# Key convolution of a delta head moved into the tail of the head before it, query gate and value taps moved ahead of the inversion

## The chip, the cores and the metric

The kernel runs on one core of one Trainium2 chip. The metric is the device time of one execution in microseconds (us). In what follows TensorE is the matmul engine (PE in the rows, PEld its weight loads), VectorE is DVE, ScalarE is ACT, and SP is the queue that issues the weight transfers.

## The reference

One step of a two-layer hybrid model in float32, for 1024 prompt tokens and 8 sample tokens (1032 columns here). Layer 0 mixes with four gated-delta heads and four retention heads, layer 1 with four mLSTM heads; each layer ends with a squared-ReLU MLP. The change touches the delta heads alone:

```python
proj = xn @ w_in
conv_out = silu(causal_conv(qkv_a, conv_buf, w_conv))      # 4 taps per channel
q, k, v = split(conv_out); q = l2norm(q) * DK**-0.5; k = l2norm(k)
beta = sigmoid(b_raw); log_alpha = -exp(a_log) * softplus(a_raw + dt_bias)
# per chunk of tokens, g = cumsum(log_alpha):
a_mat = I + (k*beta @ k.T) * decay_strict;  u, w = solve(a_mat, [v*beta, k*beta*exp(g)])
qk = (q @ k.T) * decay_causal
# over the chunks, with the state S:
v_new = u - w @ S;  o = (q*exp(g)) @ S + qk @ v_new;  S = S*exp(g_last) + k_dec.T @ v_new
o = rmsnorm(o, gdn_gain) * silu(g_a)
```

## The kernel before

**Work and its order.** Everything is laid out with channels on the 128 partitions and tokens along the free dimension. A projection tile is one 128-channel output, 8 blocks of 128 input channels deep, in three thirds of 344 tokens. The weights and inputs are split in a high and a low part, so one step (one block of one third) is three matmuls, and a tile is 24 steps. Each third fills one of three banks of `PJ`, and VectorE drains it (`project_steps`, L851); a third may start only when the third three before it is drained. After a tile's last third VectorE splits the weights of a later tile (L804, the cast, and L807, the low part).

**Heads and weaving.** Layer 0 has eight units: delta heads are units 0 to 3, retention heads 4 to 7. While unit u is computed, TensorE also runs the four tiles v of u, then gate, k and q of u+1: 96 steps. They fill the places at which the head's generator yields. `DELTA_FILL` says how many steps run at each named place, and the same names and numbers let VectorE's `weave` work out after which place a third is due (one per 8 steps). Each engine has one instruction queue in program order. Engines tell each other by counting semaphores: `to_act`, `to_dve`, `to_pe` and `act_to_pe`, each waited for by the next number (`n.awaited`). A plain `n.awaited(to_dve)` only counts one signal past.

**Banks.** Five more PSUM banks carry everything else. TensorE's `claim(b, reader)` waits until the bank's last reader has emptied it; `publish` hands it over; the reader's `take` and `done` answer.

**The front of a delta head, before.** TensorE puts row sums of the gates into banks 1, 2, 4, 3 and 0 and yields `start`, `keys conv`, `keys gate` (7, 10 and 8 steps). It then waits for ScalarE's squares of k, sums them over the partitions into banks 1, 2 and 4 (L409), puts masked row sums into banks 3 and 0 (L428 and L432), and yields `keys norm` (11 steps). Then it waits for the normalised k, forms k·k per chunk (L422) and transposes k (L419). VectorE meanwhile does k's three older taps (`conv(1)`: L966 three times, L970), the output gate (L962), `silu(1)` (L981), q's taps, the k scaling (L1004), and LT from k·k (L1008). ScalarE does the newest tap of k and q (L1654), the gate's tanh (L1664), the decays (L1660) from banks 1 and 2, k's tanh (L1668), small exps from bank 4 (L1671, L1672), k's squares (L1674), a table load (L1675), the exps of banks 3 and 0 (L1678), and the reciprocal root of the sums (L1586, L1589).

**The inversion.** Seven levels; at each, TensorE makes two halves of level products, two of block products and two of transposes, with VectorE masking or copying after each (L1082, L1101, L1111). VectorE puts into it `silu(0)` after level 1's masks, v's three taps around levels 1 and 2, and q's scaling and products at levels 3 and 4. No projection steps are placed inside.

**The tail.** After the scan over the chunks TensorE yields `rows`, `output` and `outer` (7, 10 and 11 steps) around a sample outer product. VectorE adds it to the sample state (L1196); then it normalises and gates the head's output (L1210, L1211). ScalarE stores both states (L1618). The next head begins on ScalarE with a wait that VectorE releases, then one for both stores to have landed, then the load of the next state (L1650) and the newest tap of k.

## Time and profile before

| | |
|---|---|
| median of 3 runs | 2789.54 us (2787.52 to 2790.8) |
| profiled execution, its own time | 2787.88 us |
| its span, first to last instruction | 2785.9 us |
| TensorE busy | 2719.1 us, 98% of the span |
| VectorE busy | 1550.8 us, 56% |
| ScalarE busy | 433.0 us, 16% |
| mean granted TensorE clock | 0.992 of full |

The delta heads lie between 59 and 491 us of the span, about 108 us each. Head 0 starts at 59.2 us, and the outer products that close heads 0, 1, 2 and 3 start at 166.0, 274.9, 383.0 and 491.2 us. TensorE is counted busy while any matmul is in flight.

### The profile page before, as it was taken

The page shows a single profiled execution, that of the slowest core. Times are in us where ns is not written, and L with a number is a line of the kernel's source. Part 1 is how long each engine was busy: PE and PEld are TensorE (multiplying, and loading weights), DVE is VectorE, ACT ScalarE, POOL GpSimd, SP SyncE. Part 2 cuts the span into 40 slices and gives each one's busy share as a digit, 9 for nine tenths or more (in the row PEclk, how much of TensorE's full clock was granted, in tenths as well). Part 3 has the DMA queues.
Part 4 walks back from the last instruction along what each step waited for, and adds up shares of the span by engine and source line. Part 5 has one row for each costly group of instructions (what it writes and reads, how often), then busy time and mean ns, then how long its engine had stood idle before and what let it go on. Part 6 is the DMA issues. An engine that isn't in the chain of part 4 may idle for free. (4 is left out here: it accounts for less than half of the span.)

```text
span 2785.9 us, 41603 instructions
## 1 busy us (share of the span) xinstructions
PE 2719.1 (98%) x17354; PEld 2644.0 (95%) x17354; DVE 1550.8 (56%) x2850; ACT 433.0 (16%) x894; POOL 0.2 (0%) x4
## 2 busy tenths in 40 slices
PE   8999999999899999999999999999999999999998
PEld 8888888899899999999999999999899999999998
DVE  8665765556676355364466535445675264462563
ACT  5451442222230000000001121223220000000001
POOL 0000000000000000000000000000000000000000
PEclk9999999999999999999999999999999999999999
DMA  3010011111211111111112112102311111111111
GB/s 139 16 40 17 31 47 39 52 60 60 100 41 47 53 46 46 46 46 49 48 49 92 61 38 71 68 27 77 116 40 52 46 46 46 46 46 53 46 61 61
DMA packets 44986, 150.94 MB, mean 54 GB/s; under 512 B 6024, under 2 KB 11016, under 8 KB 43792
## 3 DMA queue, kind: packets, MB, share of 16 engines
q1 hardware_dynamic: 33984, 115.42, 12.4%
q10 hardware_dynamic: 10832, 32.99, 3.2%
q8 instruction: 138, 2.26, 0.3%
q14 instruction: 32, 0.26, 0.0%
HBM read 130.32 MB, written 18.08 MB: 53 GB/s over the span
## 5 line engine op out<-in xcount | busy, mean ns | idle before, releaser
L351 PE MATMUL proj<-x_hi,w_hi 128*128 128x344 f32 x4572 | 1489.8, 326 | 18.2 <-DVEq L859 8.4
L351 PE MATMUL proj<-x_hi,w_lo 128*128 128x344 f32 x4572 | 1464.3, 320 | 0.0
L351 PE MATMUL proj<-x_lo,w_hi 128*128 128x344 f32 x4572 | 1463.7, 320 | 0.0
L351 PEld LDWEIGHTS proj<-x_hi,w_hi 128*128 128x128 f32 x4572 | 863.8, 189 | 33.6 <-issue 25.6
L351 PEld LDWEIGHTS proj<-x_lo,w_hi 128*128 128x128 f32 x4572 | 863.4, 189 | 1.7
L351 PEld LDWEIGHTS proj<-x_hi,w_lo 128*128 128x128 f32 x4572 | 863.3, 189 | 0.0
L1381 DVE TENSOR_TENSOR h<-h,proj 128x344 f32<-128x344 f32 x144 | 73.8, 512 | 372.3 <-PE proj L351 372.3
L807 DVE TENSOR_TENSOR w_lo<-w_raw,w_hi 128x1024 fp32r<-128x1024 f32 x195 | 239.0, 1226 | 7.9 <-DVE state L1147 0.7
L1366 DVE TENSOR_TENSOR mlp_t<-proj,rbc 128x344 f32<-128x344 f32 x192 | 99.0, 515 | 237.8 <-PE proj L351 224.1
L422 PE MATMUL bank<-s,s 128*128 128x128 f32 x1096 | 141.4, 279 | 14.8 <-DVE s L1040 4.5
L422 PEld LDWEIGHTS bank<-s,s 128*128 128x128 f32 x1096 | 129.3, 192 | 25.5 <-DVEq L785 8.9
L851 DVE TENSOR_TENSOR s<-proj,rbc 128x344 f32<-128x344 f32 x156 | 78.8, 513 | 118.2 <-PE proj L351 115.2
L804 DVE CAST w_hi<-w_raw 128x1024 fp32r<-128x1024 f32 x195 | 134.0, 687 | 4.3 <-DVE state L1147 1.2
L1596 ACT ACTIVATE ssq<-h 128x344 f32<-128x344 f32 x9 | 4.3, 481 | 635.6 <-DVE h L894 635.6
L1371 DVE TENSOR_TENSOR x_lo<-mlp_u,x_hi 128x344 fp32r<-128x344 f32 x192 | 99.4, 517 | 6.6
L1368 DVE SCALAR_TENSOR_TENSOR mlp_u<-mlp_t 128x344 f32<-128x344 f32 x192 | 99.3, 517 | 6.6
L1874 ACT ACTIVATE ssq<-h 128x344 f32<-128x344 f32 x3 | 1.4, 481 | 630.7 <-DVE h L1352 630.7
L1370 DVE CAST x_hi<-mlp_u 128x344 fp32r<-128x344 f32 x192 | 65.3, 340 | 6.5
L419 PE MATMUL bank<-consts,s 128*128 128x128 f32 x416 | 57.3, 277 | 6.2 <-DVEq L785 5.7
L419 PEld LDWEIGHTS bank<-consts,s 128*128 128x128 f32 x416 | 46.0, 141 | 13.7 <-DVEq L785 11.5
L1721 ACT ACTIVATE s<-bank 128x128 f32<-128x128 f32 x64 | 17.8, 278 | 258.5 <-PE bank L422 258.5
L966 DVE SCALAR_TENSOR_TENSOR s<-s,vec,s 128x1021 f32<-128x1021 f32 (+2 forms) x36 | 45.3, 1258 | 3.4 <-ACT s L1654 2.3
(323 smaller groups left out, 2021.8 us busy)
## 6 DMA issues: line engine op xcount, KB each, us to landing
w_raw<-w_all SPq DMA_DIRECT2D x204, 512.0 KB, 3.5
h<-x SPq DMA_DIRECT2D x8, 516.0 KB, 9.3
h<-x ACTq DMA_DIRECT2D x8, 516.0 KB, 6.9
h_spill<-h ACTq DMA_DIRECT2D x8, 516.0 KB, 2.6
h<-h_spill ACTq DMA_DIRECT2D x8, 516.0 KB, 5.6
y<-h SPq DMA_DIRECT2D x24, 172.0 KB, 1.9
sample_C<-state_c ACTq DMA_DIRECT2D x4, 1024.0 KB, 6.9
s_state_c<-sample_C ACTq DMA_DIRECT2D x4, 1024.0 KB
```

What stands on the lines that cost most here:

```text
L351: last = nc.tensor.matmul(PJ[:, tt, 0:TT], w[slot][:, k, :], x[:, k, tt * TT:(tt + 1) * TT], start=(at == 0 and j == 0), stop=(at == len(o ...
L419: per_chunk(b, reader, half, lambda o, c: nc.tensor.transpose(o, chunk(src, c), ident))
L422: return nc.tensor.matmul(o, l, r, start=start, stop=stop)
L804: nc.vector.tensor_copy(hi[:], src).then_inc(w_hi_done, 1)
L807: tt_(lo[:], src, hi[:].bitcast(F32), ALU.subtract).then_inc(w_split, 1)
L851: return tt_(third(dst, tt), ps, third(rbc, tt), ALU.mult)
L966: return stt(dst[:, sh:SEQ], src[:, 0:SEQ - sh], vcol(w + i), dst[:, sh:SEQ], ALU.mult, ALU.add)
L1366: drain(t, tt, lambda ps, tt: tt_(T_third[:], ps, third(rbc, tt), ALU.mult), g)
L1368: step(stt(U_third[:], T_third[:], 0.0, T_third[:], ALU.max, ALU.mult))
L1370: step(nc.vector.tensor_copy(hi, U_third[:]))
L1371: tt_(lo, U_third[:], hi.bitcast(F32), ALU.subtract).then_inc(x_ready, 1)
L1381: drain(t0 + 8 + c, tt, lambda ps, tt: tt_(hh, hh, ps, ALU.add), g)
```

## The change

Between the heads, the newest tap and the three older taps of the next head's k are done in the tail of the head ahead (head 0 still does its own at its front). The output's normalising and gating move from behind the sample outer product to in front of it, and for that VectorE waits there for the reciprocal root. Inside a head, ScalarE takes k's squares before the decays and small exps instead of after them, and q's tanh comes in front of the table load, the exps of banks 3 and 0 and the reciprocal root of k. `silu(0)`, v's newest tap, v's three older taps and q's squares go in front of the inversion; q's norm sums move from level 2 to level 1, its scaling and decayed product from level 3 to 2, and the q·k product from level 4 to 3. The fill becomes 14 steps at `start`, 10 at `keys conv`, 4 at `keys gate` and 8 at `keys norm`; TensorE's wait for k's squares now stands behind `start`, its k·k behind `keys gate`, and `keys norm` comes after the transposes of k. The diff:

```diff
@@ -68,7 +68,7 @@
-DELTA_FILL = {"start": 7, "keys conv": 10, "keys gate": 8, "keys norm": 11, "keys": 0, "invert": 1,
+DELTA_FILL = {"start": 14, "keys conv": 10, "keys gate": 4, "keys norm": 8, "keys": 0, "invert": 1,
               "level 0": 0, "level 1": 0, "block": 0, "turn": 0, "scan": 1, "state": 2, "residual": 1, "values": 1,
@@ -457,15 +457,14 @@
                     yield "start"
-                    yield "keys conv"
-                    yield "keys gate"
                     pe.wait_ge(*n.awaited(act_to_pe))
...
                         publish(hide_later(b), b)
-                    yield "keys norm"
+                    yield "keys conv"
+                    yield "keys gate"
                 else:
@@ -477,6 +476,7 @@
                         turned((4, 3)[half], "act", k, half)
+                    yield "keys norm"
                     yield "keys"
@@ -488,10 +488,10 @@
                             per_chunk(half, "dve", half, lambda o, c: mm(o, chunk(LT, c), chunk(Dm, c)))
-                        if lv == 2:
+                        if lv == 1:
                             pe.wait_ge(*n.awaited(act_to_pe))
                             over_partitions(ones, s[10], "act", (2, 4, 3))
-                        if lv == 4:
+                        if lv == 3:
                             pe.wait_ge(*n.awaited(to_pe))
@@ -961,20 +961,20 @@
-                def tap(x, i, src, dst):
+                def tap(x, i, src, dst, h=h):
                     w, sh = V_CONV + 4 * (x * HEADS + h), 3 - i
...
-                def earlier_rows(x, dst):
+                def earlier_rows(x, dst, h=h):
                     at = V_HIST + 3 * (x * HEADS + h) * NB
...
-                def conv(x):
+                def conv(x, h=h):
                     src, dst = s[x], s[4 + x]
...
                     for i in range(3):
-                        step(tap(x, i, src, dst))
-                    earlier_rows(x, dst).then_inc(*n.made(to_act))
+                        step(tap(x, i, src, dst, h))
+                    earlier_rows(x, dst, h).then_inc(*n.made(to_act))
@@ -990,23 +990,32 @@
                     q, k, vs, OT = s[4], s[5], s[6][:, SEQ:TOK], s[6]
-                    conv(1)
+                    if h == 0:
+                        conv(1)
+                    n.awaited(to_dve)
+                    gate()
+                    silu(1).then_inc(*n.made(to_act))
                     yield "start"
-                    gate()
-                    n.awaited(to_dve)
-                    silu(1).then_inc(*n.made(to_act))
-                    yield "keys conv"
                     for i in range(3):
...
                     earlier_rows(0, q).then_inc(*n.made(to_act))
+                    yield "keys conv"
+                    all_drained(T_AB + 4 * unit + 3)
+                    tell(to_act)
+                    silu(0).then_inc(*n.made(to_act))
                     yield "keys gate"
...
                     tt_(k[:], k[:], s[12][:], ALU.mult).then_inc(*n.made(to_pe))
+                    v.wait_ge(*n.awaited(to_dve))
+                    for i in range(3):
+                        step(tap(2, i, s[2], s[6]))
+                    step(earlier_rows(2, s[6]))
                     yield "keys norm"
...
                         tell(to_pe)
+                    tell(to_act)
                     yield "keys"
@@ -1074,7 +1083,6 @@
                     n.settle()
-                    all_drained(T_AB + 4 * unit + 3)
                     for lv in range(1, LEVELS):
@@ -1083,14 +1091,10 @@
                             yield "block"
-                        if lv == 1:
-                            silu(0).then_inc(*n.made(to_act))
                         if lv == 2:
-                            step(tap(2, 1, s[2], s[6]))
-                        if lv == 3:
                             v.wait_ge(*n.awaited(to_dve))
                             step(stt(q[:], q[:], QSCALE, s[10][:], ALU.mult, ALU.mult))
-                        if lv == 4:
+                        if lv == 3:
                             for half in range(2):
@@ -1114,13 +1118,7 @@
                                 yield f"level {half}"
-                        if lv == 1:
-                            v.wait_ge(*n.awaited(to_dve))
-                            step(tap(2, 0, s[2], s[6]))
                         if lv == 2:
-                            step(tap(2, 2, s[2], s[6]))
-                            earlier_rows(2, s[6]).then_inc(*n.made(to_act))
-                        if lv == 3:
                             tt_(s[10][:], q[:], s[7][:], ALU.mult).then_inc(*n.made(to_pe))
@@ -1188,6 +1186,14 @@
                     step(ts_(s[9][:, 0:NB * P], s[9][:, 0:NB * P], consts[:, K_RG + h:K_RG + h + 1], None, ALU.mult))
+                gain = vcol(V_GDN if delta else V_RET)
+                if delta:
+                    if h < HEADS - 1:
+                        all_drained(T_AB + 4 * unit + 5)
+                        tell(to_act)
+                    v.wait_ge(*n.awaited(to_dve))
+                    step(tt_(OT[:], OT[:], s[12][:], ALU.mult))
+                    step(stt(MIX[:, unit, :], OT[:], gain, MIX[:, unit, :], ALU.mult, ALU.mult))
                 yield "outer"
@@ -1195,8 +1201,12 @@
-                gain = vcol(V_GDN if delta else V_RET)
+                if delta:
+                    if h < HEADS - 1:
+                        all_drained(T_AB + 4 * unit + 6)
+                        tell(to_act)
+                        conv(1, h + 1)
+                    return
                 if unit == 2 * HEADS - 1:
@@ -1477,8 +1487,9 @@
             for u in range(2 * HEADS):
-                all_drained(T_AB + 4 * u + 3 - LATE[0])
-                tell(to_act)
+                if u == 0 or u >= HEADS:
+                    all_drained(T_AB + 4 * u + 3 - LATE[0])
+                    tell(to_act)
                 if u < 2 * HEADS - 1:
@@ -1648,7 +1659,7 @@
                 a.dma_start(s[9][:, 0:NB * P], io["state_a" if delta else "state_b"][h]).then_inc(state_in, 16)
-                def newest_tap(x):
+                def newest_tap(x, h=h):
                     act(convo[:, x * HEADS + h, 0:3 + NB], s[x][:, SEQ - 3:TOK], ACT.Copy)
@@ -1660,23 +1671,30 @@
-                    newest_tap(1).then_inc(*n.made(to_dve))
+                    if h == 0:
+                        newest_tap(1).then_inc(*n.made(to_dve))
+                    newest_tap(0).then_inc(*n.made(to_dve))
                     act(s[16][:], s[3][:], ACT.Tanh, scale=0.5).then_inc(*n.made(to_dve))
-                    newest_tap(0).then_inc(*n.made(to_dve))
-                    decays(s[17], 1, 0)
                     a.wait_ge(*n.awaited(to_act))
                     act(s[12][:], s[5][:], ACT.Tanh).then_inc(*n.made(to_dve))
+                    a.wait_ge(*n.awaited(to_act))
+                    act(s[12][:], s[5][:], ACT.Square).then_inc(*n.made(act_to_pe))
+                    decays(s[17], 1, 0)
                     decays(s[17], 2, 1)
...
                     a.wait_ge(*n.awaited(to_act))
-                    act(s[12][:], s[5][:], ACT.Square).then_inc(*n.made(act_to_pe))
+                    act(s[10][:], s[4][:], ACT.Tanh).then_inc(*n.made(to_dve))
                     nc.scalar.preload_act_table_set(LNEXP)
...
                     rsqrt_of_banks(s[12], 1.0, to_dve, banks=(1, 2, 4))
+                    a.wait_ge(*n.awaited(to_act))
+                    newest_tap(2).then_inc(*n.made(to_dve))
+                    a.wait_ge(*n.awaited(to_act))
+                    act(s[10][:], s[4][:], ACT.Square).then_inc(*n.made(act_to_pe))
                     decays(s[11], 3, 0)
@@ -1689,12 +1707,6 @@
                         last.then_inc(*done(b))
-                    a.wait_ge(*n.awaited(to_act))
-                    act(s[10][:], s[4][:], ACT.Tanh).then_inc(*n.made(to_dve))
-                    newest_tap(2).then_inc(*n.made(to_dve))
-                    a.wait_ge(*n.awaited(to_act))
-                    act(s[10][:], s[4][:], ACT.Square).then_inc(*n.made(act_to_pe))
-                    nc.scalar.preload_act_table_set(LNEXP)
                     rsqrt_of_banks(s[10], 1.0, to_dve, banks=(2, 4, 3))
@@ -1737,6 +1749,9 @@
                 rsqrt_of_banks(s[12], 1.0 / DK, to_dve, by_third=midway is not None)
+                if delta and h < HEADS - 1:
+                    a.wait_ge(*n.awaited(to_act))
+                    newest_tap(1, h + 1).then_inc(*n.made(to_dve))
                 a.wait_ge(*n.awaited(to_act))
```

## Rows read from the trace of the kernel before

**Rows 1.** The page's first part: an engine's busy time, share and instructions.

```profile
PE 2719.1 (98%) x17354; PEld 2644.0 (95%) x17354; DVE 1550.8 (56%) x2850; ACT 433.0 (16%) x894; POOL 0.2 (0%) x4
```

**Rows 2.** TensorE's waits, 60 to 494 us: total us, times, longest us.

```profile
PE bank L419 <- DVEq L785: 5.7, 20, 0.5
PE bank L422 <- DVEq L785: 5.1, 12, 0.6
PE bank L422 <- DVE s L1074: 3.9, 4, 1.0
```

**Rows 3.** Timeline of TensorE, head 0: start, length, instruction, count, idle before.

```profile
62.23 0.39 PE L351 MATMUL proj<-x_hi,w_hi 128*128 128x344 f32 x1 [1.12 <-DVE s L851]
...
74.10 1.90 PE L409 MATMUL bank<-s,consts 128*128 128x344 f32 x6
75.57 0.65 PE L428 MATMUL bank<-row_parts,row_pick 100*128 100x512 f32 x1
...
76.78 0.32 PE L351 MATMUL proj<-x_hi,w_hi 128*128 128x344 f32 x1
...
81.97 1.95 PE L422 MATMUL bank<-s 128*128 128x128 f32 x16
...
87.57 4.08 PE L422 MATMUL bank<-s,s 128*128 128x128 f32 x32 [0.96 <-DVE s L1074]
```

**Rows 4.** Timeline of ScalarE, head 0, from the decays to k's reciprocal root.

```profile
70.53 1.12 ACT L1660 ACTIVATE s<-bank,neg_g 128x128 f32<-128x128 f32 x4
...
72.00 1.07 ACT L1674 ACTIVATE s<-s 128x1032 f32<-128x1032 f32 x1 [0.21 <-DVE s L981]
73.09 1.28 ACT L1675 ACT_TABLE_LOAD   x1
74.38 1.08 ACT L1678 ACTIVATE s<-bank 128x512 f32<-128x512 f32 x2
...
76.82 1.07 ACT L1589 ACTIVATE s<-s 128x1032 f32<-128x1032 f32 x1
```

**Rows 5.** Timeline of VectorE, head 0, from silu of k to LT.

```profile
70.73 1.23 DVE L981 SCALAR_TENSOR_TENSOR s<-s,s 128x1032 f32<-128x1032 f32 x1
71.89 0.93 DVE L851 TENSOR_TENSOR s<-proj,rbc 128x344 f32<-128x344 f32 x2
72.73 3.91 DVE L966 SCALAR_TENSOR_TENSOR s<-s,vec,s 128x1021 f32<-128x1021 f32 x3
76.68 0.17 DVE L970 TENSOR_TENSOR s<-s,vec 128x8 f32<-128x8 f32 x1
...
79.07 0.69 DVE L804 CAST w_hi<-w_raw 128x1024 fp32r<-128x1024 f32 x1
79.79 1.23 DVE L807 TENSOR_TENSOR w_lo<-w_raw,w_hi 128x1024 fp32r<-128x1024 f32 x1
...
83.95 0.69 DVE L1008 TENSOR_TENSOR s<-bank,s 128x512 f32<-128x512 f32 x1 [0.20 <-PE bank L422]
```

**Rows 6.** Timeline of ScalarE, from head 0's stores to head 1's gate tanh.

```profile
168.79 0.35 ACTq L1618 DMA_DIRECT2D s_state_a<-s  x1
...
172.26 0.35 ACTq L1650 DMA_DIRECT2D s<-state_a  x1
...
175.23 1.07 ACT L1664 ACTIVATE s<-s 128x1032 f32<-128x1032 f32 x1
```

**Rows 7.** Windows: length, busy us and instructions per engine, clock, DMA share, GB/s.

```profile
171.50:172.20 0.70, 0.70 (x4) 0.70 (x4) 0.67 (x2) 0.00 (x0) 0.00 (x0) 0.50 0.00 0
504.19:507.60 3.41, 1.16 (x8) 0.90 (x7) 3.34 (x4) 0.33 (x1) 0.00 (x0) 1.00 0.00 0
507.60:511.01 3.41, 3.41 (x14) 3.41 (x13) 3.31 (x5) 0.00 (x0) 0.00 (x0) 0.50 0.01 2
```

**Rows 8.** Timeline of TensorE, head 1: first projection step, first norm sum.

```profile
169.61 0.42 PE L351 MATMUL proj<-x_hi,w_hi 128*128 128x344 f32 x1
...
182.94 1.90 PE L409 MATMUL bank<-s,consts 128*128 128x344 f32 x6
```

## The prediction

> **What bounds the kernel now.** I read the page first: TensorE is busy 98% of the span, VectorE 56%, ScalarE 16% [rows 1]. So a change gains only where TensorE stands idle, and loses wherever it makes TensorE stand. Next I read TensorE's waits over the four delta heads. The three kinds that the change can touch hold 14.7 us in all: 5.7 and 5.1 us in short waits between inversion steps, and 3.9 us in four waits of about 1 us at the start of level 0 [rows 2]. No wait of that list stands in the front of a head before level 0. Last come the timelines of the front on the three engines [rows 3 to 5] and of the seam between two heads [rows 6 to 8]. They show why the front has no wait: the 25 projection steps of head 0 end at 74.10, and ScalarE's squares of k ended at 72.00 + 1.07 = 73.07, one microsecond earlier. The exps that free banks 3 and 0 end at about 74.9 and 75.46, and TensorE needs bank 3 at 75.57 [rows 3, 4]. The old order is just in time.
>
> **Durations.** A projection step is (74.10 - 62.23) / 25 = 0.475 us. The norm sums and masked row sums behind them take 76.78 - 74.10 = 2.68 us [rows 3].
>
> **Removed from the inversion.** `silu(0)` (1.23 us), three taps of v and their small add leave VectorE's share of it. They stand at two places, and I give each the longest wait of its kind: 0.5 us in front of a turn, 0.6 us in front of a block product [rows 2]. That is 1.1 us a head. The norm sums, the scaling and the q·k product move up a level with their waits. Sum: -4.5 us over four heads. This is all the gain inside the heads, since what is removed from an engine that is 56% or 16% busy counts only through these waits.
>
> **First stall: k's squares and the five banks.** TensorE now waits behind 14 steps, not 25. In head 0, k's convolution stays where it is, so the squares still end at 73.07. TensorE arrives at 62.23 + 14 x 0.475 = 68.88. The wait does not end with the squares. The new sums go into banks 1, 2 and 4, whose decays and small exps ScalarE now reads after the squares: two groups of four decays at 1.12 us or a little less [rows 4], and the small exps, to about 75.4. Behind them TensorE needs banks 3 and 0 again, and ScalarE empties these only behind q's tanh, which waits for q's taps. On VectorE these follow `silu(1)`, ended 71.96: one third drained (0.4 us), then 4.1 us of taps and add [rows 5], so tanh starts at about 76.45. Tanh 1.07, table load 1.29, then exps of 0.54 each [rows 4]: bank 3 is free at 79.4, bank 0 at 79.9, and the last row sums are issued by about 80.45. So TensorE goes on 7.4 us after the squares' end. Lost: 80.45 - 68.88 - 2.68 = 8.9 us.
>
> For heads 1 to 3 I start from ScalarE, the later of two paths. The k taps in the tail begin when VectorE has added the outer products, about when the store is issued at 168.79 [rows 6], and end 4.1 us later, at 173.0. ScalarE must still issue two stores and see them land before it loads the next state. Before, a VectorE signal held it to 172.26 [rows 6]. No DMA traffic is left after 171.50 [rows 7], so I take 171.5 for the load. From load to the gate's tanh is 175.23 - 172.26 = 2.97 us, since one newest tap stands there as before. Tanh, gate, `silu(1)` and squares follow each other: 1.07 + 1.23 + 1.23 + 1.07 and four hand-overs of about 0.04. The squares end at about 179.2. TensorE arrives at 169.61 + 6.65 = 176.26 [rows 8] and goes on at 179.2 + 7.4 = 186.6. Lost: 186.6 - 176.26 - 2.68 = 7.7 us a head. If the stores allowed no earlier load, it would be 8.4; if they landed 1 us earlier, 6.7.
>
> **Second stall: k's scaling.** Between there and k·k lie 14 steps, 6.65 us. VectorE must first drain the third that ends 10 steps in, because v must be complete before it tells ScalarE and does `silu(0)`. The third 0.52, its settling about 0.15, `silu(0)` 1.23, a weight cast of 0.69 due at that place, the scaling 1.23 (the length of `silu`, same shape) [rows 5]: 3.8 us. k is ready 4.75 + 3.8 = 8.55 us after TensorE went on, so 1.9 us are lost. The reciprocal root is not late: from the first exp to its end is 76.82 + 1.07 - 74.38 = 3.5 us [rows 4], so it ends at 82.4 in head 0, before the scaling at about 87.7.
>
> **Third stall: LT.** From k·k to the end of the second LT transpose, with two steps between, TensorE needs 87.57 - 0.96 - 81.97 = 4.64 us [rows 3], now with 8 steps more, 8.4 us. VectorE needs v's taps and add 4.1, the low part of a weight tile 1.2, a third 0.4, the first half of LT and its settling 0.9, and from the second half to level 0 another 87.57 - 83.95 = 3.6 [rows 3, 5]: 10.2 us. The wait grows from 0.96 to 1.8: 0.85 us more.
>
> **The clock.** In the stretch 504.19 to 507.60 TensorE had 1.16 us of work, and in the next 3.41 us the granted clock was 0.50, the lower of its two levels, 1.2 GHz [rows 7]. Head 1 began at that level: its 25 steps took 13.33 us where head 0's took 11.87, and the clock was 0.50 there too, so one such stretch costs 1.46 us [rows 3, 7, 8]. Each first stall leaves TensorE idler than that, and the 14 steps behind it hold up the third on which `silu(0)` waits. I take one stretch a head. In head 1 the old stretch then falls in front of the stall, where it costs nothing, so there the two cancel. Bounds: none (-1.46 x 3), or one more in each head behind the second and third stalls, which are near 1.9 us each (+5.8).
>
> **Sum.** Head 0: 8.9 + 1.9 + 0.85 + 1.46 = 13.1. Head 1: 7.7 + 1.9 + 0.85 = 10.4. Heads 2 and 3: 11.9 each. Together 47.3; less 4.5 in the inversion; less 0.4 at unit 4, where the same early end of VectorE's tail lets ScalarE start between 0 and 0.76 us earlier. +42.4 us. The output's gating in the tail costs nothing: two passes of `silu`'s size, some 2.5 us [rows 5], delay one drain by at most their own length, and the third that needs that bank comes 8 steps, 3.8 us, into the next head. The profiled execution took 2787.88 us, so 2830.3. It lay 1.7 us below the median of 2789.54; I predict 2831.
>
> **A rule to weigh.** ScalarE loads a table six times a head before and four times after; a load takes 1.28 us, and the squares end 0.02 us before one starts [rows 4]. The Trainium skill ("ScalarE: Activation LUTs", What ACT_TABLE_LOAD costs, and Table sets: the hidden batching unit) wants functions of one set grouped, and puts a switch at 2.66 us with a drain of 1.38. The trace shows no such drain.
>
> **The rivals.**
> - *The stalls as computed*, 2831 us, its own range 2822 to 2840.
> - *The fill hides the second and third stalls*: VectorE, freed by the long first stall, would have k and LT ready. Against it: both hang on work that TensorE makes after the first stall, the third at step 24 and k·k. Then 4 x (1.9 + 0.85) = 11 us less: 2820.
> - *The clock falls for more than one stretch each time*, three a head: 4 x 2 x 1.46 = 12 us more, 2843. For it: after a first stall of 8 us at least two stretches are idle. Against it: the half clock during idleness costs nothing, only what follows does.
> - *It does what its name says and is faster.* If k's squares came before TensorE's 14th step and the banks were free by then, only the 4.5 + 0.4 us of gains would stay: 2784.6. It is decided at one point: the squares' end at or before 176.3 in head 1, and the exps of banks 3 and 0 in time. The path I found ends 2.9 us too late for the squares, and 8 for the banks.
> - *ScalarE's table loads set the pace.* If ScalarE's chain were what TensorE waits for through the whole head, eight loads fewer would give 8 x 1.28 = 10.2 us: 2779. Against it: ScalarE is 16% busy [rows 1]. By the Trainium skill's 2.66 us a switch (same page) it would be 21 us, 2768.
>
> **How the numbers follow.** Chances: stalls as computed 0.72, later stalls hidden 0.09, more of the low clock 0.12, faster as named 0.04, table loads 0.01, and 0.02 that gains and losses cancel within 0.2%, 5.6 us, which is about what a measurement of this kernel can tell from no change. Faster 0.05, same 0.02, slower 0.93. The two cases on the fast side stay outside the range; it takes in the bounds of the clock and of the stores: 2818 to 2843.
>
> **What would show it.** In the profile of the changed kernel: per delta head a wait of 5 us or more before a norm sum at L409's counterpart and another of some 3 us before the masked row sums, released by ScalarE's exps; one of about 1.9 us before k·k; level 0's wait near 1.8 us; the two inversion waits of 0.5 and 0.6 gone; the clock at 0.50 behind each first stall. The forecast is wrong if banks 3 and 0 are free when TensorE comes, or if TensorE's busy time grows as its waits do not.

## The result, and the profile after

The changed kernel takes 2828.05 us (median of 4 runs, 2824.78 to 2832.48), the one before 2789.59 (4 runs, 2787.52 to 2790.80). The ratio is 1.0141, 95% interval 1.0125 to 1.0157: 38.5 us slower, where 2831 was forecast, in a range of 2818 to 2843. The profiled execution took 2827.59 us, its span is 2825.8 (before: 2785.9, so +39.9), and the mean granted clock of TensorE is 0.988 (before 0.992).

The page's first part of the changed kernel, the counterpart of [rows 1]:

```profile
PE 2728.6 (97%) x17354; PEld 2647.9 (94%) x17354; DVE 1552.8 (55%) x2850; ACT 422.7 (15%) x886; POOL 0.2 (0%) x4
```

ScalarE's eight instructions fewer are table loads. TensorE has as many instructions as before, and 9.5 us more busy time. Its waits from 60 to 530 us, the four delta heads, in the columns of [rows 2]:

```profile
PE bank L409 <- ACT s L1671: 15.7, 4, 5.2
PE bank L422 <- DVE s L1008: 7.5, 4, 1.9
PE bank L428 <- ACT s L1692: 6.9, 4, 2.3
PE bank L422 <- DVE s L1083: 6.5, 4, 1.6
PE bank L419 <- DVEq L785: 5.3, 20, 0.7
...
PE bank L422 <- DVEq L785: 2.6, 8, 0.4
```

The first three lines are new and the fourth was 3.9: 36.6 - 3.9 = 32.7 us of new waits, all in front of level 0. The inversion's two kinds went from 5.7 and 5.1 to 5.3 and 2.6: 2.9 us less. 32.7 + 9.5 - 2.9 = 39.3 of the 39.9 us. The 9.5 us of busy time are a part of the loss too: the same matmuls took longer where the granted clock was 0.50, as the next timeline shows.

Timeline of TensorE in head 0, against [rows 3]:

```profile
62.64 0.39 PE L351 MATMUL proj<-x_hi,w_hi 128*128 128x344 f32 x1 [1.13 <-DVE s L851]
...
74.64 3.75 PE L409 MATMUL bank<-s,consts 128*128 128x344 f32 x6 [5.16 <-ACT s L1671]
79.89 0.50 PE L428 MATMUL bank<-row_parts,row_pick 100*128 100x512 f32 x1 [1.49 <-ACT s L1692]
...
80.94 0.32 PE L351 MATMUL proj<-x_hi,w_hi 128*128 128x344 f32 x1
...
89.59 2.05 PE L422 MATMUL bank<-s 128*128 128x128 f32 x16 [1.89 <-DVE s L1008]
...
99.75 2.29 PE L422 MATMUL bank<-s,s 128*128 128x128 f32 x16 [1.63 <-DVE s L1083]
```

The reader sees the three stalls of the forecast in their order: 5.16 + 1.49 us before the norm sums and the masked sums, 1.89 before k·k, 1.63 before level 0. The six norm sums between the two parts of the first stall took 3.75 us, where they took 1.90 in [rows 3]. No wait stands between them, and each took 0.78 us instead of 0.45: the clock was at 0.50, as the windows below show. So the first stall is larger than its idle time. That the norm sum into bank 1 waits for L1671, decays, and not for the squares themselves, is seen on ScalarE (head 0, against [rows 4]):

```profile
72.41 1.06 ACT L1681 ACTIVATE s<-s 128x1032 f32<-128x1032 f32 x1 [1.38 <-DVE s L981]
73.38 2.16 ACT L1671 ACTIVATE s<-bank,neg_g 128x128 f32<-128x128 f32 x8
...
76.86 1.06 ACT L1688 ACTIVATE s<-s 128x1032 f32<-128x1032 f32 x1 [1.20 <-DVE s L970]
77.94 1.28 ACT L1689 ACT_TABLE_LOAD   x1
79.24 1.08 ACT L1692 ACTIVATE s<-bank 128x512 f32<-128x512 f32 x2
```

The squares end at 73.47. Behind them come eight decays out of the banks that the norm sums want, q's tanh with its wait for VectorE, a table load, and only then (L1692) the exps that free banks 3 and 0. VectorE's part in the second stall and the third (head 0, against [rows 5]):

```profile
85.86 0.52 DVE L851 TENSOR_TENSOR s<-proj,rbc 128x344 f32<-128x344 f32 x1 [3.26 <-PE proj L351]
86.56 1.23 DVE L981 SCALAR_TENSOR_TENSOR s<-s,s 128x1032 f32<-128x1032 f32 x1 [0.19 <-DVEq L785]
87.71 0.69 DVE L804 CAST w_hi<-w_raw 128x1024 fp32r<-128x1024 f32 x1
88.31 1.23 DVE L1008 TENSOR_TENSOR s<-s,s 128x1032 f32<-128x1032 f32 x1
89.46 3.91 DVE L966 SCALAR_TENSOR_TENSOR s<-s,vec,s 128x1021 f32<-128x1021 f32 x3
...
95.17 1.52 DVE L1016 TENSOR_TENSOR s<-bank,s 128x512 f32<-128x512 f32 x2
```

k's scaling (L1008) stands behind the drain that waits for v's last third, `silu(0)` and the cast; LT (L1016) stands behind v's three taps.

The seam to head 1 on ScalarE, against [rows 6]:

```profile
179.89 0.35 ACTq L1629 DMA_DIRECT2D s_state_a<-s  x1
...
183.83 0.35 ACTq L1661 DMA_DIRECT2D s<-state_a  x1
...
186.79 1.07 ACT L1677 ACTIVATE s<-s 128x1032 f32<-128x1032 f32 x1
...
190.43 1.06 ACT L1681 ACTIVATE s<-s 128x1032 f32<-128x1032 f32 x1 [1.61 <-DVE s L981]
```

From the store's issue to the load's it takes 3.94 us here and 2.97 in the two other seams (before: 172.26 - 168.79 = 3.47, and there a signal of VectorE came last; the stores had landed 2.91 us after the issue). From the load to the end of the squares it takes 191.49 - 183.83 = 7.66.

Where the clock fell (windows of the changed kernel, columns as in [rows 7]):

```profile
71.45:78.25 6.80, 3.60 (x6) 1.80 (x6) 5.27 (x6) 4.63 (x13) 0.00 (x0) 0.50 0.00 0
...
194.30:197.70 3.40, 1.32 (x3) 0.31 (x1) 0.52 (x2) 2.79 (x3) 0.00 (x0) 0.50 0.02 5
197.70:201.10 3.40, 3.19 (x9) 2.81 (x10) 0.00 (x0) 3.02 (x6) 0.00 (x0) 0.50 0.00 0
```

In head 0 the clock is at its lower level, 1.2 GHz, only within the stall, and full again when TensorE goes on at 80.94. In head 1 it still holds when TensorE goes on. Head 1's front, in the ledger below, is 2.4 us longer than head 3's: 0.97 us come from the later landing of the stores, 0.82 from masked sums and 0.6 from the steps behind them at half clock. In head 2, which is 1.9 us longer than head 3, it is the half clock alone (0.82 and 1.13).

A ledger for the rest, read off the timelines by head. Head 0 begins with its first row sum, heads 1 to 3 with the outer products that close the head before (some 2 us earlier than their first row sum). The rows 2 to 4 are counted from that point; a "front" ends at level 0, the "inversion and after" goes from there to the next head:

| | before, heads 0 to 3 | after, heads 0 to 3 |
|---|---|---|
| head begins (us) | 59.24, 166.00, 274.86, 383.01 | 59.66, 177.09, 296.40, 415.27 |
| TensorE goes on behind the masked sums | 17.54, 19.63, 18.91, 18.91 | 21.28, 22.69, 21.70, 20.90 |
| k·k | 22.73, 24.81, 24.10, 24.11 | 29.94, 31.94, 31.48, 29.55 |
| front | 28.33, 30.42, 29.71, 29.72 | 40.09, 42.09, 41.62, 39.69 |
| inversion and after | 78.43, 78.44, 78.44, 78.44 | 77.35, 77.23, 77.25, 77.24 |
| behind the four heads | 2294.77 | 2293.60 |

Fronts +45.3, inversions -4.7, the rest -1.2, the start of head 0 +0.4: +39.9.

The line "behind the four heads" warns of something. All work there is the same in every kernel, but for unit 4's start, and still it took 2294.77 us before, 2293.60 in the changed kernel and 2289.9 to 2295.0 in the others. At unit 4's start the changed kernel gains 0.2 us. Most of the rest is how often and how long the clock falls far behind: near 2000 us of the span it is at 0.50 for 6.8 us before, for 3.4 us in the changed kernel, and not at all in its variants of runs 1 to 6. So the spans of those six variants are 1.4 to 3.1 us shorter than the changed kernel's where nothing was edited.

### The profile page after: what moved, and what is told of

It is laid out like the page before. It is cut to its first block and busy times, and to the rows that moved or that the text cites. A ratio compares the mean times of both kernels' runs of the same rounds, so it can differ in the third digit from the quotient of the medians.

```text
span 2825.8 us, 41602 instructions
## 1 busy us (share of the span) xinstructions
PE 2728.6 (97%) x17354; PEld 2647.9 (94%) x17354; DVE 1552.8 (55%) x2850; ACT 422.7 (15%) x886; POOL 0.2 (0%) x4
## 5 line engine op out<-in xcount | busy, mean ns | idle before, releaser
L351 PEld LDWEIGHTS proj<-x_hi,w_hi 128*128 128x128 f32 x4572 | 864.4, 189 | 32.7 <-issue 24.1
L409 PE MATMUL bank<-s,consts 128*128 128x344 f32 x96 | 36.8, 525 | 15.8 <-ACT s L1671 15.7
```

Source lines behind the costliest of these rows:

```text
L351: last = nc.tensor.matmul(PJ[:, tt, 0:TT], w[slot][:, k, :], x[:, k, tt * TT:(tt + 1) * TT], start=(at == 0 and j == 0), stop=(at == len(o ...
```

## The experiments

Eleven kernels. Unless said otherwise, each is the changed kernel with the edit shown. Ratios are against the kernel before on the same chip (2788 to 2789 us). Lengths per head are those of the ledger. The interval of a ratio is some 4 us to either side, 2.5 where 10 or 11 runs were taken; the eleven were timed on three chips, apart from the changed kernel.

**1. The exps of banks 3 and 0 before q's tanh.**

```
                     act(s[8][:, SEQ:TOK], ps[:, NB:2 * NB], ACT.Exp).then_inc(*done(4))
-                    a.wait_ge(*n.awaited(to_act))
-                    act(s[10][:], s[4][:], ACT.Tanh).then_inc(*n.made(to_dve))
-                    nc.scalar.preload_act_table_set(LNEXP)
                     for half, b in enumerate((3, 0)):
                         ps = take(b)
                         act(chunk(s[7], 4 * half, 4), ps[:], ACT.Exp).then_inc(*done(b))
+                    a.wait_ge(*n.awaited(to_act))
+                    act(s[10][:], s[4][:], ACT.Tanh).then_inc(*n.made(to_dve))
+                    nc.scalar.preload_act_table_set(LNEXP)
```

> The changed kernel, with the exps that empty banks 3 and 0 put in front of q's tanh instead of behind it and the table load. Theory (banks 3 and 0 hold TensorE until 7.4 us after the squares' end): TensorE goes on about 4 us after the squares' end, the wait before the masked row sums goes, and all that follows comes 3.5 us earlier in each head: 4 x 3.5 = 14 us less than 2828, about 2814. Rival (the front hangs on q's taps and tanh and on the reciprocal root, which stay where they are): under 3 us less, 2825 or more.

Measured: 2818.54 us, ratio 1.0105 (1.0089 to 1.0120), 9.5 us less than the changed kernel. The wait before the masked sums is gone from the list (it was 6.9), and TensorE goes on 1.9 to 2.5 us earlier in each head, at 19.18, 20.79, 19.19 and 19.03. The order on ScalarE is a cause, then, worth 8.4 us at that point. The rest of the expected gain did not arrive for a reason that I had not counted, the clock. Norm and masked sums are on the path now, and at 0.50 they took 4.19, 5.21, 4.59 and 4.43 us instead of 2.68, 7.7 us in sum:

```profile
74.22 3.41 PE L409 MATMUL bank<-s,consts 128*128 128x344 f32 x6 [5.17 <-ACT s L1671]
77.21 0.66 PE L428 MATMUL bank<-row_parts,row_pick 100*128 100x512 f32 x1
...
191.49 3.78 PE L409 MATMUL bank<-s,consts 128*128 128x344 f32 x6 [3.65 <-ACT s L1671]
194.56 1.13 PE L428 MATMUL bank<-row_parts,row_pick 100*128 100x512 f32 x1
```

And one more stretch at half clock now begins 28 to 31 us into each head, between k·k and LT. k·k to level 0 takes 11.5 us instead of 10.15. At level 0 the four fronts are 4.7 us shorter in sum; 3.1 of the 8.2 us by which the span is shorter lie behind the four heads.

**2. 25 steps ahead of the norm sums instead of 14.**

```
-DELTA_FILL = {"start": 14, "keys conv": 10, "keys gate": 4, "keys norm": 8,
+DELTA_FILL = {"start": 25, "keys conv": 0, "keys gate": 3, "keys norm": 8,
```

> The changed kernel with its fill alone altered: 25 steps at start, 0 at keys conv, 3 at keys gate, 8 at keys norm. Theory (TensorE comes too early because only 14 steps stand in front of the squares): it comes 5.2 us later and loses that much less at the first stall; three thirds are then drained before q's taps, which gives back about 1 us, and k's scaling comes when the reciprocal root is done. Level 0 starts about 4.2 us earlier in each head: 17 us less than 2828, about 2811, still over 0.5% slower than before. Rival (the order on ScalarE is the whole loss, wherever the steps stand): 2825 or more. Rival (the steps are the whole loss): near 2790.

Measured: 2816.76 us, ratio 1.0098 (1.0083 to 1.0113), 6 us more than expected and between the two rivals. TensorE's waits of this kernel, same stretch and columns:

```profile
PE bank L428 <- ACT s L1692: 21.7, 4, 5.4
PE bank L422 <- DVE s L1083: 5.6, 4, 1.4
```

The wait for the squares and the one for k's scaling are gone, but a new one of 5.4 us a head stands in front of the masked sums. Placed at "start", 25 steps bring with them the drain of the third that TensorE makes with its 24th step, and that drain stands ahead of q's taps on VectorE. So q's tanh, and behind it the exps of banks 3 and 0, come only then. Of the 15.7 + 6.9 + 7.5 = 30.1 us of the first two stalls, 21.7 were there again under another line.

**3. k's scaling ahead of the drain of v's third, `silu(0)` and the cast.**

```
                     yield "keys conv"
+                    n.awaited(to_dve)
+                    v.wait_ge(*n.awaited(to_dve))
+                    tt_(k[:], k[:], s[12][:], ALU.mult).then_inc(*n.made(to_pe))
                     all_drained(T_AB + 4 * unit + 3)
...
-                    v.wait_ge(*n.awaited(to_dve))
-                    tt_(k[:], k[:], s[12][:], ALU.mult).then_inc(*n.made(to_pe))
```

> The changed kernel, with k's scaling on VectorE put in front of the drain of v's last third, of silu(0) and of the weight cast, instead of behind them. Theory (the second stall of 1.9 us is that drain, silu(0) and the cast): it goes in each head, and the third stall grows by less than half of it: 4 to 8 us less than 2828, 2820 to 2824. Rival (k hangs on its reciprocal root): 2828.

Measured: 2829.07 us, ratio 1.0148 (1.0133 to 1.0164): no gain at all. A miss for my number. TensorE's waits of this kernel:

```profile
PE bank L409 <- ACT s L1672: 14.4, 4, 4.2
PE bank L422 <- DVE s L1084: 8.8, 4, 2.2
PE bank L428 <- ACT s L1693: 8.0, 4, 2.9
```

The second stall is gone as a wait, so its cause is confirmed. Of its 7.5 us, 2.3 went over to the wait before level 0 (6.5 to 8.8), and most of the rest into the clock. In head 0 it is at 0.50 for 10.2 us instead of 6.8, now also on the masked sums and the steps behind them, and the front got 1.65 us longer. Heads 1 to 3 each have a stretch at 0.50 that falls on the inversion, which takes 78.92, 78.63 and 78.80 us instead of 77.25: 4.6 us more in sum, against fronts only 0.8 us shorter in sum. Behind the four heads the run is 3.1 us shorter without having been edited there.

**4. TensorE kept busy through the first stall.** 30 matmuls without use ahead of the norm sums and 6 ahead of the masked sums, into a part of PSUM that is free there; they compute nothing that is read.

```
+                    for _ in range(30):
+                        nc.tensor.matmul(PJ[:, 2, 0:TT], w_hi[0][:, 0, :], XA[0][:, 0, 0:TT], start=True, stop=True)
```

> The changed kernel with extra work: in each delta head 30 matmuls in front of TensorE's wait for k's squares and 6 behind the norm sums, into a bank that the next third overwrites. They fill the idle time of the first stall and nothing else. Theory (the stalls are ScalarE's and VectorE's, and the low clock behind them adds a few us): the same waits in sum, but the clock stays at its upper level in the front; 3 to 6 us less than 2828, 2822 to 2825. Rival (the clock is no part of the loss): 2828. Rival (TensorE was not waiting): 30 more matmuls of 0.16 us in each head, 20 us more.

Measured: 2828.11 us, ratio 1.0141 (1.0125 to 1.0156). A miss. The waits before the norm and masked sums fell to 2.9 and 4.4 us (in heads 0 and 2 the added matmuls left none before the norm sums), and the time at half clock in the four heads from about 34 to 17 us. But the loads of the states followed their stores after 4.77, 4.92 and 5.14 us instead of 3.94, 2.96 and 2.97. That is 5 us of delay at the point that sets the squares of heads 1 to 3. The run does not bound what the clock costs, because the landing of the stores changed with it; why they landed later stays open.

**5. v's three older taps back at levels 1 and 2 of the inversion.**

```
                     tt_(k[:], k[:], s[12][:], ALU.mult).then_inc(*n.made(to_pe))
-                    for i in range(3):
-                        step(tap(2, i, s[2], s[6]))
-                    step(earlier_rows(2, s[6]))
...
+                            step(tap(2, 1, s[2], s[6]))
...
+                            step(tap(2, 0, s[2], s[6]))
...
+                            step(tap(2, 2, s[2], s[6]))
+                            earlier_rows(2, s[6]).then_inc(*n.made(to_act))
```

> The changed kernel with v's three older taps back at levels 1 and 2 of the inversion, the other parts as changed. Theory of the prediction: the taps in front of LT cost 0.85 us in each head (the wait before level 0 is 1.63 in the changed kernel and 0.96 in the one before) and save 0.5 to 0.6 in the inversion, so nothing that counts: 2827 to 2830, front 0.7 shorter and inversion 0.6 longer. Rival: the taps in front hold VectorE enough to feed the long stalls: 2822 or less.

Measured: 2837.82 us, ratio 1.0188 (1.0173 to 1.0204), 10 us slower than the changed kernel. Both numbers missed. The front got only 0.4 us shorter in head 0 (40.09 to 39.68), and the inversion 3.2 to 3.7 us longer (80.60, 80.80, 80.96, 80.46 against 77.35, 77.23, 77.25, 77.24). Moved up a level with `silu(0)` in front, q's scaling stands at level 2, and the taps now stood beside it: a wait of 1.70 us opened there in every head, and one of 1.35 in three of them. So the taps in front are the right part of this change, once q's scaling has moved up.

**6. The changed kernel in another order.** Edits 1 and 2 together, and q's three taps ahead of the drains that belong to the first 25 steps.

```
-                    yield "start"
                     for i in range(3):
                         step(tap(0, i, s[0], q))
                     earlier_rows(0, q).then_inc(*n.made(to_act))
+                    yield "start"
                     yield "keys conv"
```

> The changed kernel with three moves of order and nothing else: the exponentials of banks 3 and 0 in front of q's tanh on ScalarE, 25 of the 36 steps of projection ahead of the squares' norm sums, and q's three older taps on VectorE in front of the drains that belong to those 25 steps. Theory: the whole loss is order. Neither the squares (7.4 us) nor the masked sums (5.4 us in the version with 25 steps) are waited for then, 28 steps of work stand where before had them, and level 0 begins some 31 to 33 us into a head as against 28.3 to 29.7 in before; with the inversion 1.2 us a head shorter, 2790 to 2797. Rival: what is left of the loss is not order but the longer chain of VectorE in front of the inversion (v's three taps and silu(0) there), and another wait of 4 to 7 us a head opens on k's scaling or on the drains: 2810 or more.

Measured: 2797.11 us, ratio 1.0031 (1.0019 to 1.0043). That is 31 of the 38.5 us, 29.3 of them in the fronts. Fronts are 33.04, 34.97, 32.65 and 33.51, the inversions unchanged at 77.35, 77.25, 77.23 and 77.24. Its waits from 60 to 530 us (1.8 of the 10.9 us lie behind the four heads):

```profile
PE proj L351 <- DVE s L851: 10.9, 6, 2.8
PE bank L422 <- DVE s L1083: 5.6, 4, 1.4
...
PE bank L422 <- DVE s L1008: 2.9, 4, 1.0
```

What is left is now on VectorE: drains that come late behind q's taps, LT behind v's taps, k's scaling. The 25 steps ahead of the norm sums cover ScalarE's chain again, as in the old order.

**7. The tail part alone**, in the kernel before: the next head's k taps behind the outer products, its newest tap on ScalarE, the output's gating ahead of them. 

```
+                if delta:
+                    if h < HEADS - 1:
+                        all_drained(T_AB + 4 * unit + 6)
+                        tell(to_act)
+                        conv(1, h + 1)
+                    return
...
+                if delta and h < HEADS - 1:
+                    a.wait_ge(*n.awaited(to_act))
+                    newest_tap(1, h + 1).then_inc(*n.made(to_dve))
```

> The kernel before with one part of the change alone: the next head's k is convolved in the tail and the output's gating stands in front of the outer products. Front, inversion and fill stay. Theory (TensorE has no wait in the front of a head before, so an earlier k is worth nothing; a little is gained at unit 4): 2789.1, no difference that can be measured. Rival (the move itself costs, by the drain it delays or by a longer tail): 2 us or more a head, 2796 or more. Rival (it is where a gain lies): 2784 or less.

Measured: 2787.01 us, ratio 0.9991 (0.9982 to 1.0001). Fronts 28.34, 30.44, 28.90 and 30.48, in sum as before, inversions 78.46 to 78.51. Neither gain nor loss: the old front had no wait that an earlier k could close.

**8. In the kernel before, 9 steps at "keys norm" and 2 at each "invert"** instead of 11 and 1.

```
-DELTA_FILL = {"start": 7, "keys conv": 10, "keys gate": 8, "keys norm": 11, "keys": 0, "invert": 1,
+DELTA_FILL = {"start": 7, "keys conv": 10, "keys gate": 8, "keys norm": 9, "keys": 0, "invert": 2,
```

> The kernel before with its fill alone altered: 9 steps at keys norm and 2 at each invert, instead of 11 and 1. Theory (level 0 waits 0.96 us for VectorE's chain from LT, and k's scaling has 2.8 us to spare): two steps come behind k·k, the wait nearly goes, 4 x 0.95 = 3.8 us less than before, about 2785.5. Rival (k is late when its product comes 0.95 us earlier): no difference, 2789.

Measured: 2784.32 us, ratio 0.9985 (0.9976 to 0.9994). As expected: the wait before level 0 is gone, and the fronts of heads 0, 1 and 3 become 0.9 to 1.6 us shorter, that of head 2 by 0.2.

**9. Tail part, and q, `silu(0)` and v's taps in front for heads 1 to 3**, with 25 steps in front of the norm sums and edit 8. VectorE's front in these heads:

```
+                        conv(0)
+                        yield "start"
+                        gate()
+                        silu(1).then_inc(*n.made(to_act))
+                        yield "keys conv"
+                        silu(0).then_inc(*n.made(to_act))
+                        yield "keys gate"
+                        all_drained(T_AB + 4 * unit + 3)
+                        tell(to_act)
+                        v.wait_ge(*n.awaited(to_dve))
+                        for i in range(3):
+                            step(tap(2, i, s[2], s[6]))
+                        step(earlier_rows(2, s[6]))
                     v.wait_ge(*n.awaited(to_dve))
                     tt_(k[:], k[:], s[12][:], ALU.mult).then_inc(*n.made(to_pe))
```

> A version meant to keep the gains without the stalls. Like the kernel before with the tail's part, and in heads 1 to 3 q's taps first, decays, small exps and the exps of banks 3 and 0 all in front of TensorE's need, silu(0) and v's taps in front of the inversion, 25 steps before the norm sums as before; in all delta heads 9 steps at keys norm and 2 at each invert instead of 11 and 1. Head 0 keeps silu(0) and v's taps in its inversion. Theory: 3 x 1.1 us from the inversion, 4 x 0.95 from level 0's wait, 0.4 at unit 4: 7.5 us less than before, about 2782. Banks 3 and 0 and k's scaling come just in time; if either is late it costs up to 1 us a head, 2785. Rival (the inversion's waits come back elsewhere): 2789.

Measured: 2787.10 us, ratio 0.9997 (0.9988 to 1.0006). A miss by 5 us. TensorE waits 1.64, 1.64 and 1.37 us for k's scaling and 1.01 for LT. The inversion's 1.2 us a head are paid back in the front. VectorE's timeline in head 1 says what held the scaling:

```profile
188.50 0.17 DVE L970 TENSOR_TENSOR s<-s,vec 128x8 f32<-128x8 f32 x1
189.41 1.24 DVE L1019 TENSOR_TENSOR s<-s,s 128x1032 f32<-128x1032 f32 x1 [0.74 <-ACT s L1619]
```

v's taps had ended 0.7 us before; the last to come was k's reciprocal root (L1619), which on ScalarE stood behind v's newest tap and q's squares.

**10. As 9, but v's taps left in the inversion**, v's newest tap and q's squares behind k's reciprocal root on ScalarE, and 8 and 9 steps instead of 7 and 10 at "start" and "keys conv".

```
                         all_drained(T_AB + 4 * unit + 3)
                         tell(to_act)
-                        v.wait_ge(*n.awaited(to_dve))
-                        for i in range(3):
-                            step(tap(2, i, s[2], s[6]))
-                        step(earlier_rows(2, s[6]))
                     v.wait_ge(*n.awaited(to_dve))
```

> The tail's part, the fill of 9 and 2, and for heads 1 to 3 q's taps and silu(0) in front, banks 3 and 0 emptied in front of the table load, but v's taps left in the inversion; 8 steps at start and 9 at keys conv, so that the first third is drained in time. Theory: what made the combined version's k late by 1.6 us was v's tap and q's squares in front of k's reciprocal root, and VectorE busy with v's taps; without them 3 x 0.54 from silu(0)'s wait, 4 x 0.95 from level 0's wait and 0.4 at unit 4 are left: 5.8 us less than before, about 2783. Rival (the front of heads 1 to 3 is full on VectorE with or without v's taps): 2787.

Measured: 2783.31 us (11 runs), ratio 0.9982 (0.9973 to 0.9991). The inversions of heads 1 to 3 take 78.0 us, 0.6 less than head 0's. The waits for k's scaling and LT are gone; since both moves were made at once, the run does not tell what each is worth. One new wait, 1.41 us in heads 1 and 3, stands before the norm sums.

**11. As 10, with three steps moved from behind the norm sums to ahead of them.**

```
-DELTA_FILL = {"start": 8, "keys conv": 9, "keys gate": 8, "keys norm": 9,
+DELTA_FILL = {"start": 8, "keys conv": 9, "keys gate": 11, "keys norm": 6,
```

> The tail part, q's gate in front for heads 1 to 3 and 2 steps at each join of the inversion, as in the best version so far, but 28 steps of projection instead of 25 ahead of the squares' norm sums and 6 instead of 9 behind them. Theory: in heads 1 to 3 TensorE waited 1.41 us for the squares, and k's scaling was ready 2.2 us before it was asked for, so three steps moved across close the wait at no cost: 3 x 1.4 = 4.2 us, 2779. Rival: the scaling of k then comes too late (as in the combined version, 1.64 us a head) or low clock falls on work instead of on the wait: 2783 or more.

Measured: 2784.39 us, ratio 0.9986 (0.9977 to 0.9995), and its span equals that of run 10, 2780.9. The rival was right. The wait for the squares is gone, and two others appeared, 0.30 us before k·k and 0.90 before level 0 in head 1. VectorE's chain had no slack behind the one on ScalarE. So run 10 is the best median found, 5 us under the kernel before. Run 8 alone gives 4 us of that with an edit that is no part of the change, and the intervals of runs 8, 10 and 11 overlap: that parts of the change add anything to it is not shown.

## Why the prediction was right, step by step

**First stall.** Computed for head 0: TensorE goes on 7.4 us after the squares' end, and 8.9 us are lost. Measured: 80.94 - 73.47 = 7.47, and 21.28 - (2.98 + 6.65) - 2.68 = 8.97. The parts that made it up (eight decays, q's tanh behind q's taps, one table load, two exps) stand in the rows in that order. Runs 1, 2 and 6 show it by taking it apart: ScalarE's order alone gives back 2.1 us of it, and the eleven steps moved behind it give back the rest only with that order mended and with q's taps ahead of the drain that comes with those steps. The stall looks other than forecast in one point: the waits before the norm sums were 5.16, 3.65, 2.66 and 4.21 us, not 5 or more in every head, because a part of the time went by as norm sums at half clock.

**Heads 1 to 3.** From load to squares' end 7.7 us were computed, 7.66 measured. The stores' landing was the uncertain term: 2.7 us taken, 3.94, 2.97 and 2.97 measured. The middle value was 0.3 us short, and one seam lies outside the bounds I gave. TensorE went on 8.29, 8.28 and 7.47 us behind the squares' end, for 7.4 computed; in heads 1 and 2 the masked sums ran at half clock.

**Second stall.** 1.9 us computed. Measured 1.89, behind the instructions that were named; run 3 took that wait away by moving k's scaling ahead of them. It was not 7.5 us of gain, though: what stands next (LT) took some of it, the clock the rest.

**Third stall.** 0.96 to 1.8 us computed, 1.63 measured. The two inversion waits: 4.5 us computed, 4.7 measured. Run 5 shows that this small sum held only as a package: with q's scaling moved up and the taps left behind, the inversion takes 2.0 to 2.5 us a head more than in the kernel before, instead of 1.2 less.

**The clock** was the term that was most mis-sized. I took one stretch of 1.46 us on the projection steps behind each first stall, net 4.4 us. It was to be at 0.50 behind each of them, and was so only in heads 1 and 2. The 14 steps there took 0, 0.6, 1.1 and 0 us longer than at full clock, 1.7 us in sum, and in heads 1 and 2 the masked sums were about 0.8 us slower. That is roughly 3.3 us, since most of the low clock fell in time when TensorE stood anyway. Terms of the sum against measured: fronts 47.3 and 45.3, inversion -4.5 and -4.7, unit 4 -0.4 and -0.2, in all +42.4 and +39.9. The -0.6 that is missing in this list (+0.4 ahead of head 0, -1.0 far behind the heads) is no part of the forecast's mechanism; without it the forecast would be 2.0 us off instead of 2.5.

**The rivals.** That the fill hides the second and third stalls is refuted by their 7.5 and 6.5 us. That the clock falls for three stretches a head on work is refuted for the change itself. That the change is faster as named was decided where it was said, at the squares and the banks. Run 6 meets that condition nearly and still ends 9 us slower, because VectorE is then late: the rival's price, 2784.6, had left out the three taps and `silu(0)` in VectorE's front. Table loads: eight fewer and 10.3 us less ScalarE time, in a kernel that took 38.5 us longer, so they do not set the pace; what they are worth by themselves no run shows.

Open: why the stores land after 2.97 us in some seams and 3.94 to 5.14 in others, and how much of run 4's loss is the landing. The 3.94 us are tied to the seam from head 0 to head 1: the ten kernels with the new tail other than run 4's have 3.92 to 3.95 us there and 2.96 to 2.99 in the next two.

## What to carry to other kernels

Work moved ahead of a wait must be followed on each engine that reads in order: here it put ScalarE's emptying of banks 3 and 0 behind a tanh that VectorE fed, and three more behind the squares, and cost nine times what it saved (45.3 us against 4.9). Count how many steps of cover stand in front of each handoff, and keep that count when the handoff moves; a fill table tuned for one order is wrong for the next, and on VectorE the same table also moves drains. When one wait is removed, look at what stands 1 us behind it: in runs 2, 9 and 11 the next wait took most of the gain, in run 3 a third. And when a difference of 3 us is read, look first whether it arises where the edit is.

## What the runs showed of the hardware

The stretches at half clock (0.50 granted, 1.2 GHz) in the delta heads lasted 3.4 to 10.2 us; the one at 194.3 us began 1.6 us after a wait of 3.65 us had ended. Where a stretch ends decides its price. In the changed kernel the 6.8 us of head 0 cost nothing on the steps behind. In run 3 a stretch of 3.4 us in each of heads 1 to 3 cost 1.4 to 1.7 us of inversion, and in run 1 one of the same length cost 1.35 us between k·k and LT. So removing 2 us of waiting can gain nothing. TensorE's busy time tells of it: 9.5 us more for the same 17354 instructions. Part of it are the norm sums, six of which took 3.75 us at 0.50 and take 1.90 in [rows 3]; where they end before the wait for bank 3, as in the changed kernel's head 0, that costs nothing, and in run 1, where that wait is gone, it does.

The same pair of stores (512 and 64 KB) let the next load go 2.97 us after the issue of the first of them in most seams, and 3.94, 4.77, 4.92 and 5.14 us in others. The 3.94 comes back in the same seam of kernel after kernel; the last three are run 4's.

A table load took 1.28 us and the next activation began 0.01 to 0.02 us after it, here as in [rows 4]. The Trainium skill ("ScalarE: Activation LUTs", What ACT_TABLE_LOAD costs) adds a drain of 1.38 us to each switch; no switch in these traces shows one.
